# Which queue waits before a buffer is used again, and when ScalarE copies the turned probabilities: a two-layer encoder trunk

## What is computed

```python
for l in range(DEPTH):                      # DEPTH = 2, SEQ = 256, D_MODEL = 2048
    h = rmsnorm(x, norm_mix[l])
    proj = h @ w_in[l]
    qa, ka, va, qi, ki, wi, qb, kb, vb = jnp.split(proj, offsets, axis=-1)
    o_a = dsa_branch(...)    # 8 heads of 128: an indexer keeps 64 keys, softmax, p @ v
    o_b = swa_branch(...)    # 16 heads of 64, window 128, learned sinks, softmax, p @ v
    gates = jax.nn.sigmoid(h @ w_gate[l])
    g_a, g_b = jnp.split(gates, 2, axis=-1)
    merged = g_a * (o_a @ w_branch_a[l]) + g_b * (o_b @ w_branch_b[l])
    x = x + merged @ w_out[l]
    h = rmsnorm(x, norm_mlp[l])
    x = x + jnp.square(jax.nn.relu(h @ w_up[l])) @ w_down[l]
return rmsnorm(x, final_norm)
```

## Time and profile before

| | before |
|---|---|
| median of 3 runs | 2658.03 us (2656.35 to 2661.28) |
| the profiled execution, its own time | 2658.03 us |
| its span, first to last instruction | 2656.1 us |
| PE, PEld (weight loads) | 2641.4 us, 2217.1 us busy |
| DVE, ACT, POOL | 2078.8 us, 1448.1 us, 215.8 us busy |
| chain that ended last | PE 95%, DVE 3%, DMA 1%, issue 1% |
| granted clock of TensorE | 0.999 |
| DMA | 594.52 MB, 224 GB/s |

### The profile page before, as it was taken

One profiled execution on the slowest core, in us unless ns is written; L12 is line 12 of the kernel. 1 busy time (PEld: TensorE's weight loads), 2 busy tenths in 40 slices (PEclk: granted clock), 3 DMA queues, 4 the chain that ended last, 5 costly groups with the idle time before them and its releaser, 6 DMA issues.

```text
span 2656.1 us, 37301 instructions
## 1 busy us (share of the span) xinstructions
PE 2641.4 (99%) x13432; PEld 2217.1 (83%) x13432; DVE 2078.8 (78%) x3099; ACT 1448.1 (55%) x1863; POOL 215.8 (8%) x378
## 2 busy tenths in 40 slices
PE   9999999999999999999999999999999999999998
PEld 7788778888888888888888887788888888888887
DVE  5667678967898897987756766789678989989875
ACT  5445555545565655655455455555456556556554
POOL 0103110000100100100010021100000001000000
PEclk9999999999999999999999999999999999999999
DMA  7877676666775766767777666667677767667574
GB/s 260 239 236 224 222 226 195 229 231 231 244 228 191 246 216 206 240 205 232 235 237 225 224 225 221 218 202 233 227 256 231 221 208 242 209 217 234 189 248 151
DMA packets 187395, 594.52 MB, mean 224 GB/s; under 512 B 25576, under 2 KB 46612, under 8 KB 187088
## 3 DMA queue, kind: packets, MB, share of 16 engines
q1 hardware_dynamic: 166256, 536.94, 62.1%
q0 software_dynamic: 20432, 54.86, 7.5%
q10 hardware_dynamic: 528, 0.37, 0.1%
HBM read 544.58 MB, written 47.48 MB: 223 GB/s over the span
## 4 chain that ended last, share of the span: by engine, by line
PE 95%; DVE 3%; DMA 1%; issue 1%; ACT 0%; DVEq 0%; POOLq 0%; POOL 0%; SPq 0%; ACTq 0%
PE acc L578 24%; PE acc L579 24%; PE acc L580 24%; PE att L546 2%; PE att L548 2%; PE att L547 2%; PE acc L546 2%; PE acc L548 2%; PE acc L547 2%; PE acc L595 1%; PE acc L594 1%; PE acc L596 1%; DMA raw<-in_w_main 1%; DVE w_lo L1350 1%; DVE w_lo L1371 1%
## 5 line engine op out<-in xcount | busy, mean ns | idle before, releaser
L1350 DVE TENSOR_TENSOR w_lo<-raw,w_hi 128x1024 fp32r<-128x1024 f32 (+1 forms) x778 | 933.2, 1211 | 374.0 <-ACT w_hi L922 370.3
L922 ACT ACTIVATE w_hi<-raw 128x1024 fp32r<-128x1024 f32 (+1 forms) x778 | 813.1, 1051 | 633.5 <-PE acc L580 462.4
L578 PE MATMUL acc<-w_hi,h_hl 128*128 128x512 f32 x1848 | 735.2, 398 | 1.1 <-DVE w_lo L1350 1.1
L580 PE MATMUL acc<-w_hi,h_hl 128*128 128x512 f32 x1848 | 728.9, 394 | 0.0
L579 PE MATMUL acc<-w_lo,h_hl 128*128 128x512 f32 x1848 | 728.6, 394 | 0.0
L578 PEld LDWEIGHTS acc<-w_hi,h_hl 128*128 128x128 f32 x1848 | 347.9, 188 | 83.0 <-issue 4.9
L580 PEld LDWEIGHTS acc<-w_hi,h_hl 128*128 128x128 f32 x1848 | 347.9, 188 | 81.3
L579 PEld LDWEIGHTS acc<-w_lo,h_hl 128*128 128x128 f32 x1848 | 348.2, 188 | 76.3
L1371 DVE TENSOR_TENSOR w_lo<-raw,w_hi 128x1792 fp32r<-128x1792 f32 x166 | 335.5, 2021 | 33.5 <-ACT w_hi L931 32.4
L578 PE MATMUL acc<-w_hi,o_hl 128*128 128x512 f32 x912 | 360.4, 395 | 0.0
L579 PE MATMUL acc<-w_lo,o_hl 128*128 128x512 f32 x912 | 360.0, 395 | 0.0
(11 more groups left out here) (298 smaller groups left out, 3614.9 us busy)
## 6 DMA issues: line engine op xcount, KB each, us to landing
raw<-in_w_main SPq DMA_DIRECT2D x928, 512.0 KB, 4.3
scratch<-spread SPq DMA_DIRECT2D x37, 512.0 KB, 2.8
moved<-scratch SPq DMA_DIRECT2D x148, 128.0 KB, 3.2
scratch<-spread POOLq DMA_DIRECT2D x30, 512.0 KB, 3.5
moved<-scratch POOLq DMA_DIRECT2D x120, 128.0 KB, 5.0
scratch_p<-spread POOLq DMA_DIRECT2D x16, 384.0 KB, 4.6
moved<-scratch_p POOLq DMA_DIRECT2D x64, 96.0 KB, 4.3
raw<-in_w_misc SPq DMA_DIRECT2D x16, 336.0 KB, 4.0
```

Source lines behind the costliest of these rows:

```text
L578: nc.tensor.matmul(o, a_hi, hi[:, kk], start=(k == 0), stop=False)
L580: last = nc.tensor.matmul(o, a_lo, hi[:, kk], start=False, stop=fin)
L922: nc.scalar.activation(w_hi[s][:, 0:2 * width], raw[r][:, 0:2 * width], ACT.Copy).then_inc(hi_ready, 1)
L1350: nc.vector.tensor_tensor(w_lo[s][:, 0:2 * width], raw[r][:, 0:2 * width], w_hi[s][:, 0:2 * width].bitcast(F32), ALU.subtract).then_inc(lo ...
```

## The change

In both mixers GpSimd no longer waits for the two buffers. DVE does so in its place, ahead of the spread: it waits until the last block of the same buffer has been fetched (`a_landed`, `probs_landed`) and taken (`probsT_ready`). The take is moved by one position: in mixer A from the visit to the position behind it, in mixer B from two positions after the visit to three. All transfers, copies and products stay the same, as does the order of the work within every other job.

```diff
             def pass_a_probs(l, h):
-                if h >= 2:
-                    pool.wait_ge(a_landed, (l * A_HEADS + h - 1) * LANDED)
                 pool.wait_ge(a_spread_out, l * A_HEADS + h + 1)
...
                 pool.wait_ge(a_stored, (l * A_HEADS + h + 1) * 16)
-                if h >= 2:
-                    pool.wait_ge(probsT_ready, l * JOBS + (h - 1))
...
             def pass_probs(l, j):
-                if j:
-                    pool.wait_ge(probs_landed, (l * B_JOBS + j) * LANDED)
                 pool.wait_ge(probs_spread, l * B_JOBS + j + 1)
...
                 pool.wait_ge(probs_stored, (l * B_JOBS + j + 1) * 16)
-                if j:
-                    pool.wait_ge(probsT_ready, l * JOBS + (A_HEADS + j))
...
                         a_exp(l, h)
-                    if 0 <= h + 1 - A_LATER < A_HEADS:
-                        a_take_probsT(l, h + 1 - A_LATER)
+                elif 0 <= h + 1 - A_LATER < A_HEADS:
+                    a_take_probsT(l, h + 1 - A_LATER)
...
-                if off == B_STEP - 2 and 0 <= j - 1 < B_JOBS:
+                if off == B_STEP - 1 and 0 <= j - 1 < B_JOBS:
                     b_take_probsT(l, j - 1)
...
             def a_spread(l, h):
                 dve.wait_ge(probs_ready, l * JOBS + (h + 1))
                 if h >= 2:
-                    dve.wait_ge(a_stored, (l * A_HEADS + h - 1) * 16)
+                    dve.wait_ge(a_landed, (l * A_HEADS + h - 1) * LANDED)
+                    dve.wait_ge(probsT_ready, l * JOBS + (h - 1))
...
             def b_spread(l, j):
                 dve.wait_ge(probs_ready, l * JOBS + (A_HEADS + j + 1))
                 if j:
-                    dve.wait_ge(probs_stored, (l * B_JOBS + j) * 16)
+                    dve.wait_ge(probs_landed, (l * B_JOBS + j) * LANDED)
+                    dve.wait_ge(probsT_ready, l * JOBS + (A_HEADS + j))
```

## The result

The changed kernel takes 2674.47 us (median of 6 runs, 2670.09 to 2675.84) against 2659.33 us before (6 runs): ratio 1.0055, 95% interval 1.0042 to 1.0067. That is 15 us slower, where 22 were forecast, 2680 us with a range of 2667 to 2697.

The account below looks back on a forecast made before the run. PE, busy 99% of the span, was taken to set the time. Mixer A's 8.9 us plus mixer B's 13.1 gave 22.0 us over the profiled 2658.03: 2680 us, range 2667 to 2697.

Parts of the forecast that it names:

- the first rival: Mixer B: spread to landing under 10.8 us, so only the gates' 2.2 us add to A's 8.9: 2669 us, chance 0.20.
- Mixer A: Takes behind one more split, emptyings, the DVE loop and last takes make PE late: 8.9 us for both layers.
- visits 4 and 8: Mixer A: an emptying ahead of the takes of visits 3 and 7 makes each 1.3 us late for PE.
- the loop through DVE at visits 4 to 6: Mixer A: loop take to take is 7.1 us against PE's 6.89, 0.2 us a visit, 0.6 a layer.
- Mixer B: Loop through HBM outlasts PE's visit: 6.6 us in a layer, 13.1 in two.
- loop of 13.8 us: Mixer B: signal, spread, landing and take, each waiting for the one before, take 13.8 us against PE's 12.90.
- spread's end to landing: Mixer B: time from spread's end until the fetch lands, taken as 11.75 us, bounds 11.33 and 12.78.
- My rival: Mixer B: loads after DVE's three splits in a row slow the store, loop 15.4 us, 2702 us, chance 0.14.
- The gate's emptying: Mixer B, visits 3 and 6: emptying before the take, hidden by the landing; uncovered 0.56 us each, 2.2 in all.
- the list of what is queued behind the waiting spread: Mixer B: DVE's splits, which shift together with PE, with room of 2.1 us.
- No second stall: Mixer B: split needed at 4.4 us, done 2.3 after the take, so PE does not wait a second time.
- signs: Expected in the changed kernel's profile: PE's take waits, product distances about 13.8 us in B, DVE and ACT idling.

Follow-up runs that it names:

- E1: Only the two takes moved, all waits as in the kernel before: 2664.15 us, ratio 1.0022 to the kernel before.
- E2: Only the waits moved from GpSimd to DVE, takes as in the kernel before: 2657.66 us, ratio 1.0000 to the kernel before.
- six other profiles named above: Profiled executions of six follow-up kernels whose code for mixer A's takes and waits is that of the changed kernel; no common time.
- E6: Changed kernel, but mixer A's takes of visits 3, 7 and 9 at their old position: 2671.19 us, ratio 1.0044 to the kernel before.
- E4: The whole change in mixer B alone, against the kernel before: 2669.05 us, ratio 1.0040.
- E9: Changed kernel with each mixer B fetch as eight transfers of 16 rows instead of four of 32: 2676.16 us, ratio 1.0058 to the kernel before.
- E11: Changed kernel with an extra 32 KB transfer, waited for, between store and fetch in mixer B: 2712.55 us, ratio 1.0205 to the kernel before.
- E3: The whole change in mixer A alone, against the kernel before: 2664.93 us, ratio 1.0026.
- E10: Kernel before with each mixer B fetch as eight transfers instead of four: 2658.36 us, ratio 0.9994 to the kernel before.
- E12: Kernel before with an extra 32 KB transfer, waited for, between store and fetch in mixer B: 2673.57 us, ratio 1.0053 to the kernel before.
- E7: Changed kernel, but mixer B's takes of visits 3 and 6 at their old position: 2670.84 us, ratio 1.0043 to the kernel before.
- E8: Changed kernel, but mixer B's job 7 guarded as before, by GpSimd's waits: 2670.12 us, ratio 1.0038 to the kernel before.

## Why the prediction was right, and where its size was off

**The direction and the cause were right.** PE waits for the takes, in both mixers, as forecast, and for nothing else that is new and large. E1 and E2 separate the two edits: the takes alone cost 6 us, the waits alone nothing, both 15. The remaining 9 us come from neither edit by itself. By the products of the profiled executions 4.2 us of them are in mixer B and 3.8 in mixer A, 2.7 of these in layer 2, where the last take varies. In mixer B E2's loop through HBM has 3 us between take and product, and in E1 the take is late but no spread waits for it; together the loop is closed with 0.6 us of room. The forecast's working needs both edits for this, but it doesn't say that the waits alone would cost nothing.

The time lies in the stated range, nearer to the 11 us of the first rival (the landing keeps up) than to the 22 of the forecast.

**GpSimd's waits.** Forecast gain 0, measured none (E2).

**Mixer A.** Forecast 8.9 us, by the products 3.0 in layer 1 and 4.0 in layer 2, 7.0 in all. For layer 1 the last product is at 262.00 against 259.14, 2.9 us, and 0.2 more because this execution was that much earlier ahead of the mixer. For layer 2, from visit 3 to the last product, it is 1587.57 - 1536.48 against 1576.29 - 1528.95, 3.8 us, and 0.3 for visit 3 itself. Visit 3's product begins 0.3 us late in each layer, as forecast, visits 4 and 8 cost 1.1 each (forecast 1.3), the last of layer 1 0.6 (forecast 0.4) and that of layer 2 1.6 (forecast 1.5). The last match is in part luck: in the six other profiles named above it is 0.2 to 1.6. The 0.6 us a layer for the loop through DVE at visits 4 to 6 did not come: the distances are 6.88 to 6.91 us. (Its terms add up to 7.17 us, not 7.1, which would have made it 0.3 us a visit.) E6 shows that the emptyings are the main cause.

**Mixer B.** Forecast 13.1 us, measured 3.5 and 2.8, 6.3. By the distances 1.7 of these are the four gate visits, 3.1 the two last products, and only 1.5 the four visits between the gates, where the forecast had its loop of 13.8 us set every visit. Here one term of the sum was mis-sized: "spread's end to landing ... I take 11.75". In the changed kernel ACT's five waited takes give 11.40, 11.19, 11.30, 10.82 and 11.23 us, mean 11.2, and E2's fourteen that waited 10.4 to 12.0, mean 11.0. Where ACT did not wait, the landing was earlier than the take: at job 6 within 10.2 and 10.1 us. I had said that this number stood for DMA behaviour under a new pattern of loads, and that 0.1 us of it was 1.4 us of the time. What changed is the store: fetch after store in the 16 jobs took 4.3 to 6.4 us before, median 4.9, and 3.0 to 4.0 in 14 jobs of the changed kernel (5.6 and 6.0 in the job 0 of each layer, whose spread does not wait). The DMA engines over the time of a store, before (316.78 to 322) and after (350.53 to 353.9), from store's issue on:

```profile
DMA  6979999692995942993599993979999999999999
...
issues: line engine op xcount, KB each, median us to landing
raw<-in_w_main SPq DMA_DIRECT2D x2, 512.0 KB, 3.8
scratch_p<-spread POOLq DMA_DIRECT2D x1, 384.0 KB, 4.1
```
```profile
DMA  0000000000000991991996990019591919797989
...
raw<-in_w_main SPq DMA_DIRECT2D x2, 512.0 KB, 3.6
scratch_p<-spread POOLq DMA_DIRECT2D x1, 384.0 KB, 3.1
```

Each digit is the busy share of a fortieth of the stretch. In the second stretch nothing is under way for the first third: DVE has stood still for 3 us, so SyncE had no buffer to load, and the store finds the DMA engines free. All runs agree with this: the store's median to landing is 2.8 to 3.2 us in the nine kernels in which DVE waits before the spreads of mixer B (the changed one, E2, E4 to E9, E11), and 4.1 to 4.6 in the five in which it doesn't (the one before, E1, E3, E10, E12). My rival had the reverse, that the burst of three splits would slow the store. The stall that the loop makes shortens the loop. What the prediction set against that rival held: the fetches behind the shorter stores take longer, a median of 4.6 us against 4.3, so that the whole way is 0.6 us shorter and not 1.8.

The Trainium skill, DMA: Bandwidth & Descriptors, Anatomy of one DMA, gives by its fit, as an estimate, 2.9 us for such a store. The 3.1 us of the second stretch are near it; before, with the weights beside it, the median in the profile was 4.6. The 2.2 us for a fetch, which the prediction quotes from the same section of the Trainium skill, did not come in either kernel. (The 4 us that the prediction takes from it are a shortening of its own loop of 13.8 us; against the visit of 12.90 that is 3 us.)

With 11.2 us the loop is 0.1 + 1.04 + 11.2 + 0.94 = 13.3, near the visits without a gate between the two gate visits of layer 1 (13.51 and 13.30) and one of the two in layer 2 (13.35; the other is 12.93). The gate's emptying, which I had hidden behind a landing of 13.8, now sets its visits (13.32 and 13.35); E7 shows that it is not hidden.

**The last visit.** The forecast's loop has the last product 1.7 us late by the landing (13.82 us against 12.17 before). The wait is there, 1.96 and 1.89 us, but ACT did not wait for the fetch. After visit 7's stall DVE comes late to the sums for the next gates, ACT waits for these to round them, and takes behind them:

```profile
394.45 0.63 ACT L1159 ACTIVATE s_hh<-stage 128x512 fp32r<-128x512 f32 x1 [4.54 <-DVE stage L1731]
...
399.98 0.63 ACT L1159 ACTIVATE s_hh<-stage 128x512 fp32r<-128x512 f32 x1 [2.73 <-DVE stage L1731]
400.52 1.04 ACT L914 ACTIVATE w_hi<-raw 128x1024 fp32r<-128x1024 f32 x1
401.46 0.92 ACT L1043 ACTIVATE probsT<-moved 128x384 f32<-128x384 f32 x2
```

E8 removes that stall and with it the wait in layer 1. This path, from DVE's stall to ACT by way of the sums, was missing from the list of what is queued behind the waiting spread. No second stall came, as forecast: PE's waits for splits went from 1.3 to 2.0 us, in four places instead of one, with 0.2 us at most in the mixers.

**The signs.** Three of the signs that the prediction named did not come as stated. PE waits for 11 takes in B and 10 in A (forecast about 14, and 12 to 14). ACT waits for the fetch in 5 takes of B, not in most. DVE waits 1.4 to 3.3 us before a spread of B, 2.4 in the mean, not 3 to 4 or more. The last two say that the loop through HBM is shorter than forecast and sets fewer visits.

**The sum.** 7.0 + 6.3 = 13.3 us of 14.4 between the two profiled spans; the other 1.1 are not traced to a place.

## What to carry to other kernels

When a wait moves from an idle queue to a busy one, write down the loop that it closes, with every engine and transfer in it, and compare its length with the distance at which the main engine asks. For the kernel before, price the single pass as well: about 3 us of room were not enough for a transfer of 3.7 (E12). A copy that an engine does between other work is late by whatever was put ahead of it: look for the visits with an extra job, not at the mean one. And don't take a DMA's duration over from a trace in which the traffic beside it was spaced otherwise: here a stall emptied the DMA engines and made the store 1.8 us and the whole way 0.6 us shorter than the trace of before had led me to take.

## What the runs showed of the hardware beyond that

Cutting a fetch of four transfers into eight of half the size cost only 0.3 us to the landing of the last in E9 and 0.6 in E10, though GpSimd issues for 4.1 us instead of 2.2. And in E11 TensorE's granted clock fell behind some of PE's waits. The granted clock (the column behind PE, PEld, DVE, ACT and POOL) around the wait of 3.65 us that ends at 340.53:

```profile
336.00:341.00 5.00, 1.79 (x8) 1.05 (x8) 0.39 (x1) 2.23 (x4) 0.64 (x2) 0.87 0.50 168
341.00:345.00 4.00, 4.00 (x20) 2.74 (x17) 4.00 (x6) 0.81 (x2) 0.57 (x1) 0.50 0.44 150
345.00:349.00 4.00, 4.00 (x16) 3.19 (x15) 1.97 (x15) 2.22 (x10) 0.56 (x1) 0.81 0.83 316
349.00:353.00 4.00, 4.00 (x19) 3.24 (x18) 2.12 (x6) 1.65 (x2) 2.21 (x4) 1.00 0.38 108
```

It is 0.50, the lower level of 1.2 GHz, from 341 to 345, and back at 2.4 GHz by 349. It is 0.50 also behind the waits of 4.53 and 4.69 us (389 to 393, 1686 to 1690), and 0.57 behind the wait of 3.23 us in E12 (1692 to 1696). Behind the waits of 1.96 and 2.11 us in the changed kernel it is 1.00 in every stretch of 4 us, and its mean over the run is 0.999. E11 took 38 us over the changed kernel, where the expectation had 28 to 34. Its loop was as expected (15.8 us); seven times 15.8 - 13.3 is already 17.5 us a layer, 35 in all. What the lower clock adds is not separated.
